# Expert stage of a hybrid mixer and mixture-of-experts layer: matmul order turned, one list for all slots, results added onto x1 in memory

## The reference, cut to what matters

```python
x = x + mod_lat[:, 2] * mix_x                                  # "x1" below
h = modulate(rms_norm(x, norm_ffn_g), mod_lat[:, 3], mod_lat[:, 4])
# router: best group by h @ rg_w + rg_b, then the two best of its four experts by h @ re_w + re_b
for e in range(16):
    y = y + gates[..., e:e + 1] * ((silu(h @ wg[e]) * (h @ wu[e])) @ wd[e])
x = x + mod_lat[:, 5] * y
out = rms_norm(x, final_norm_g)
```

## Time and profile before

| | |
|---|---|
| time, median of 3 runs | 1084.59 us (1083.99 to 1084.71) |
| the profiled execution's own time | 1086.46 us |
| its span, first to last instruction | 1084.7 us |
| mean granted TensorE clock | 0.903 |
| busy: PE, DVE, ACT, POOL | 900.0, 718.8, 415.1, 392.1 us |
| first expert matmul, last `expert_rows` store issued | 536.4, 1028.6 us |

### The profile page before, as it was taken

The page is one execution under the profiler, slowest core; times in us unless marked ns, Lnnn a source line. Parts: engine busy times, 40 slices in busy tenths (PEclk is TensorE's granted clock), DMA queues, the critical chain, the costliest instruction groups (busy, mean ns, idle before and its releaser), DMA issues.

```text
span 1084.7 us, 12383 instructions
## 1 busy us (share of the span) xinstructions
PE 900.0 (83%) x3689; PEld 632.3 (58%) x3690; DVE 718.8 (66%) x794; ACT 415.1 (38%) x520; POOL 392.1 (36%) x181
## 2 busy tenths in 40 slices
PE   6789999949798899992379998999999899988800
PEld 2354444414345478882358886888888677767700
DVE  2234778996883353446885778568646988888648
ACT  1333535325436221113242454435414556556212
POOL 1000735910000000003253647156341777766672
PEclk9989999969899999995589998999999888888955
DMA  8884405015205422316555748476452888887494
GB/s 318 292 330 135 176 20 193 0 39 187 105 0 203 184 78 112 117 78 255 188 190 212 279 168 317 159 271 238 158 223 86 317 317 309 325 311 268 168 358 190
DMA packets 96277, 213.48 MB, mean 197 GB/s; under 512 B 11007, under 2 KB 31613, under 8 KB 96253
## 3 DMA queue, kind: packets, MB, share of 16 engines
q1 hardware_dynamic: 85708, 174.37, 43.9%
q0 software_dynamic: 5904, 21.50, 5.5%
q10 hardware_dynamic: 4640, 17.30, 3.9%
HBM read 180.12 MB, written 33.03 MB: 197 GB/s over the span
## 4 chain that ended last, share of the span: by engine, by line
PE 51%; DVE 28%; issue 8%; DVEq 4%; DMA 3%; ACT 3%; POOL 2%; SPq 0%; ACTq 0%; POOLq 0%
PE bank L701 10%; DVE WP L1524 7%; PE bank L908 3%; PE bank L888 3%; PE bank L887 3%; PE bank L886 3%; PE bank L909 3%; PE bank L910 3%; PE bank L814 3%; PE bank L815 3%; PE bank L816 3%; DVE rkt L1538 2%; PE bank L745 2%; PE bank L683 2%; DVE U L1279 2%
## 5 line engine op out<-in xcount | busy, mean ns | idle before, releaser
L621 POOL TENSOR_TENSOR WP<-raw,WP 128x1024 fp32r<-128x1024 f32 x64 | 186.8, 2947 | 0.7 <-ACT WP L1138 0.5
L701 PE MATMUL bank<-hT,wring 128*128 128x512 f32 x384 | 169.3, 600 | 2.6 <-ACT hT L966 1.9
L1524 DVE TENSOR_TENSOR WP<-raw,WP 128x2048 fp32r<-128x2048 f32 x62 | 156.8, 2568 | 11.7 <-ACT WP L1134 8.3
L1134 ACT ACTIVATE WP<-raw 128x2048 fp32r<-128x2048 f32 x64 | 119.5, 1917 | 90.8 <-issue 84.9
L886 PE MATMUL bank<-WP,xp 128*128 128x512 f32 x368 | 144.1, 391 | 1.5 <-DVE xp L1561 1.5
L888 PE MATMUL bank<-WP,xp 128*128 128x512 f32 x368 | 143.8, 391 | 0.0
L887 PE MATMUL bank<-WP,xp 128*128 128x512 f32 x368 | 143.7, 391 | 0.0
L701 PEld LDWEIGHTS bank<-hT,wring 128*128 128x128 f32 x384 | 73.7, 193 | 93.5 <-issue 90.0
L617 POOL TENSOR_TENSOR held<-held 128x1 f32<-128x1 f32 x24 | 36.2, 1508 | 218.7 <-DVE idg L1553 210.8
L633 POOL TENSOR_TENSOR WP<-raw,WP 128x2048 fp32r<-128x2048 f32 x2 | 9.0, 4532 | 283.6 <-ACT WP L1134 283.6
L908 PE MATMUL bank<-WP,hp 128*128 128x512 f32 x184 | 83.2, 452 | 0.0
(11 more groups left out here) (278 smaller groups left out, 1503.6 us busy)
## 6 DMA issues: line engine op xcount, KB each, us to landing
raw<-in_expert_w_gate SPq DMA_DIRECT2D x64, 512.0 KB, 3.9
raw<-in_expert_w_up SPq DMA_DIRECT2D x64, 512.0 KB, 6.4
raw<-in_expert_w_down SPq DMA_DIRECT2D x64, 512.0 KB, 8.1
mring<-in_mod_w SPq DMA_DIRECT2D x20, 1024.0 KB, 5.3
expert_rows<-ysc ACTq DMA_DIRECT2D x23, 512.0 KB, 7.0
expert_rows<-g SPq DMA_DIRECT2D x16, 512.0 KB, 11.4
wring<-in_w_in SPq DMA_DIRECT2D x12, 512.0 KB, 6.0
mslot<-in_mod_w SPq DMA_DIRECT2D x4, 1024.0 KB, 14.9
```

The source lines that it names most:

```text
L621: pool.tensor_tensor(WP[:, j, 1, 2 * D:], raw[:, j, 2 * D:], WP[:, j, 0, 2 * D:].bitcast(F32), ALU.subtract).then_inc(s_lod[j], 1)
L701: mm = pe.matmul(o_, wring[:, n % 3, k, :], src, start=k == 0, stop=k == KD - 1)
L1134: A_(WP[:, j, 0, 0:2 * D], raw[:, j, 0:2 * D], ACT.Copy).then_inc(s_hgu, 1)
L1524: tt(WP[:, j, 1, 0:2 * D], raw[:, j, 0:2 * D], WP[:, j, 0, 0:2 * D].bitcast(F32), ALU.subtract).then_inc(s_logu[j], 1)
```

## The change

It rewrites the expert stage in five ways.

1. **Lists for all slots at once.** After the ranks are known, DVE computes each pair's slot and place, one one-hot matrix `oh` (128 x 2048 float32) and the values `rv`; 16 float32 matmuls of 70 columns give token numbers and gates of all 35 slots in one PSUM bank. From it come `gid` (rows to gather), `sid` (rows to add to; empty places point to 128 spare rows) and `gl` (gates). `prepare_slots`, `slot_ids`, `slot_gates` and `slot_numbers` are gone from the loop.
2. **PE's order is turned.** `gate_up` of slot q+1 comes before `down` of slot q:

More of the change, by code:

```diff
@@ L528, in _, with next_gate_up, next_down @@
             sp.wait_ge(s_mrow, 8)
+            def next_gate_up(e, at_e):
+                for j in range(KE):
+                    sp.wait_ge(s_logu[j], e)
+                    load_gate_up(at_e, j)
+            def next_down(e, at_e):
+                for j in range(KE):
+                    sp.wait_ge(s_lod[j], e)
+                    load_down(at_e, j)
             for j in range(KE):
@@ L532, in _ @@
                 load_down(0, j)
[L533 to L539, removed]
+            next_gate_up(1, 1)
+            next_down(1, 1)
+            next_gate_up(2, 2)
+            with sp.Fori(2, NE - 1) as e:
+                next_gate_up(e + 1, bass.ds(e + 1, 1))
+                next_down(e, bass.ds(e, 1))
+            next_down(NE - 1, NE - 1)
             for j in range(KE):
@@ L622, in split_down @@
                                    ALU.subtract).then_inc(s_lod[j], 1)
[L624 to L634, removed]
@@ L659, in _ @@
             pool.wait_ge(s_xg, 16 * W + 32)
-            hold(W)
+            scatter(W - 1, 2 * W + 1, xg[:])
+            pool.wait_ge(s_held, 4 * W + 5)
+            pool.tensor_tensor(held[:], held[:], held[:], ALU.mult).then_inc(s_held, 1)
             pool.memset(stat[:, 63:64], 0.0).then_inc(s_end, 1)
[L662 to L667, removed]
@@ L851, in _ @@
                     pe.matmul(bank[4][:, NE * i:NE * (i + 1)], (tri_b if j == i else ones_b)[:],
-                              mb[:, NE * j:NE * (j + 1)], start=j == 0, stop=j == i)
+                              mk[:, NE * j:NE * (j + 1)], start=j == 0, stop=j == i)
             for j in range(NT):
-                mm = pe.matmul(bank[5][:, 0:NE], ones_b[:], mb[:, NE * j:NE * (j + 1)], start=j == 0,
+                mm = pe.matmul(bank[5][:, 0:NE], ones_b[:], mk[:, NE * j:NE * (j + 1)], start=j == 0,
                                stop=j == NT - 1)
             mm.then_inc(s_rk, 1)
[L859 to L868, removed]
+            pe.wait_ge(s_oh, 1)
+            for n in range(2 * NT):
+                mm = pe.matmul(bank[2][:, 0:2 * NS], oh[:, n, :], rv[:, n].rearrange("p f s -> p (f s)"),
+                               start=n == 0, stop=n == 2 * NT - 1)
+            mm.then_inc(s_idx, 1)
             def turn_rows(q, r):
@@ L1143, in hi_rows @@
                    ACT.Copy).then_inc(s_xgh, 1)
-            for n in range(2):
-                act.sem_inc(s_ys[n], 16)
             for j in range(KE):
@@ L1154, in _, with early_hi, late_hi, tanh_and_rows @@
             W = act.value_load(tab[0:1, 3, 0:1], min_val=NE, max_val=MAXT)
+            def early_hi(s, E1):
+                for j in range(KE - 1):
+                    act.wait_ge(s_gud, 4 * s + j + 1)
+                    hi_gate_up(E1, j)
+            def late_hi(s, E1):
+                act.wait_ge(s_gud, 4 * s + 4)
+                hi_gate_up(E1, KE - 1)
+            def tanh_and_rows(s, nxt):
+                act.wait_ge(s_gate, s + 1)
+                A_(sg[:], bank[0][:], ACT.Tanh, scale=0.5).then_inc(s_sg, 1)
+                for r in range(2):
+                    hi_rows(s + 1, nxt, r)
@@ L1572, in _, with hidden @@
-            slot_ids(1)
-            slot_gates(1, 1)
+            def hidden(s):
+                g = gl[:, s:s + 1] if isinstance(s, int) else gl[:, bass.ds(s, 1)]
+                dve.wait_ge(s_sg, s + 1)
+                stt(out=sg[:], in0=sg[:], scalar=1.0, in1=bank[0][:], op0=ALU.add,
+                    op1=ALU.mult).then_inc(s_sil2, 1)
+                dve.wait_ge(s_sil2, s + 1)
+                dve.wait_ge(s_gud, 4 * s + 4)
+                for h in range(2):
+                    hs = slice(h * 2 * P, (h + 1) * 2 * P)
+                    stt(out=sg[:, hs], in0=bank[1][:, hs], scalar=g, in1=sg[:, hs], op0=ALU.mult,
+                        op1=ALU.mult).then_inc(s_hid, 1)
@@ L1584, in _ @@
[L1584 to L1589 removed]
+            for j in range(1, KE):
+                lo_gate_up(0, j)
+            ids1, hole = lst[:, 0], every(1500, NS)
+            link(ts(hole, ids1, 0.0, None, ALU.is_equal))
@@ new lines, in _ @@
+            link(stt(out=hole, in0=hole, scalar=K("dump"), in1=ids1, op0=ALU.mult, op1=ALU.add))
+            ts(sid[:], hole, -1.0, None, ALU.add).then_inc(s_sid, 1)
+            L0 = dve.value_load(tab[0:1, 2, 0:1], min_val=0, max_val=1)
+            E1 = dve.value_load(tab[0:1, 0, 1:2], min_val=0, max_val=NE - 1)
+            W = dve.value_load(tab[0:1, 3, 0:1], min_val=NE, max_val=MAXT)
+            with dve.If(L0 > 0):
+                for j in range(KE - 1):
+                    lo_gate_up(E1, j)
```

422 lines of the change are left out of this document (165 added, 257 removed).

## The result

The changed kernel takes 1097.76 us (median of 4 runs, 1091.22 to 1099.81), the kernel before 1084.65 in the runs beside it: a ratio of 1.011, 95% interval 1.006 to 1.015. It is slower by about 1.1 per cent, where the forecast was 3 per cent faster. The profiled execution took 1097.63.

A forecast was written before the change was run, and what follows sets the result against it. PE was taken to bound the kernel before, POOL the single slots after. Tanh of slot 14 at 796, POOL's last addition done at 1024, plus 27 gave 1051, set as 1050 us; own range 1025 to 1080, whole range 1000 to 1105.

The forecast's parts named there:

- POOL's new chain: Expert loop: POOL waits for each addition to land, so its iteration is a sum, 8 to 26.1 us by slot type.
- the iteration with a new expert after it only: POOL, expert loop: pick and gather 1.6, subtractions 9.5, addition's pick 0.6, addition 8.0, register loads 0.3; 20.0 us.
- PE bounds it: Alternating pairs of slots: 28 to 32 us on POOL against 36 on PE, so PE sets the pace.
- the 238 of the first stretch: Tanh of slot 1 to 14: 13 slots of 18.0 us, 234, plus 4 for the pair 4, 5.
- The single slot: POOL, new expert in both neighbours: 5.5 + 11.7 + 0.6 + 8.0 + 0.3 = 26.1 us, in slots 14 to 21.
- the slow addition: Rival, POOL's wait after 23 additions: landing of 13 us gives 1128, decisive from about 11.3; chance 0.25.
- The start: Before the loop: mask at 503.8, then 23.9 us to the first expert matmul at 527.7, 8.7 earlier than before.
- The tail: From tanh of slot 14 at 796: 19 us, seven iterations of 26.1, one of 20, last addition 6, ending at 1024.
- The end: After POOL's last dummy: the 16 gathers and the additions go, leaving 27 us for 52.5 before.
- A slot that PE bounds: Expert loop: `slot_numbers` goes and DVE's products are covered by `down`; 18.0 us a slot for 18.90.
- The rival with a short chain: Rival, expert loop: POOL's chain is short and PE or the transfers bound all slots; 989 us, chance 0.15.
- DVE bounds the single slots: Rival, single slots: DVE's subtractions and other work take 26 us, or 28 without overlap, giving 1066; chance 0.10.

The follow-up runs named there:

- run 5: Changed kernel, POOL's wait kept, with DVE's gate and up subtractions left out after the first expert: 1025.72 us, ratio 0.945 to the kernel before.
- run 4: Changed kernel with two more idle products of 128 x 560 on POOL after each of 22 additions: 1125.61 us, ratio 1.034 to the kernel before.
- run 8: Changed kernel with POOL waiting for an addition only before the next, and half of the down low parts moved to DVE: 1001.47 us, ratio 0.922.
- run 1: Changed kernel with POOL waiting for an addition only before it issues the next one: 1013.0 us, ratio 0.932 to the kernel before.

## Why the prediction was wrong

The sign was wrong: slower by 1.1 per cent where 3.2 per cent faster was forecast. 1097.76 lies near the upper end of the range from 1000 to 1105, and outside the 1025 to 1080 of the forecast's own case. The mechanism was named: POOL's iteration is a sum, with the landing in it. The step that failed is the sizing of that sum under "POOL's new chain", above all of the iteration with a new expert after it only, 20.0.

**The iteration with a new expert after it only.** It was 1.6 + 9.5 + 0.6 + 8.0 + 0.3 = 20.0, and measured 2.35 + 9.4 + 4.7 + 12.5 = 28.96. I gave the addition's pick 0.6, the uncontended price, and took the landing from the middle of the plain stores. But DVE has its own subtractions of the next expert just then, so both one-element operations wait out one of them (2.30 and 2.13, against 0.18 alone in run 5), and the issue takes 3.52 for 1.62. DVE's three from 579.78 to 587.72 cover all three of these operations (DVE in the changed kernel):

```profile
579.78 7.94 DVE L1523 TENSOR_TENSOR WP<-raw,WP 128x2048 fp32r<-128x2048 f32 x3 [2.97 <-ACT WP L1130]
```

Of the seven iterations before slot 14 that split a new expert's down weights, five take 27.2 to 29.0; the other two, at 655.59 and 795.32, have no subtraction of DVE beside the addition and its pick and take 20.6 and 19.2, as forecast. With the 11.55 of the other iteration (11.1 to 12.1 in four of the five between splits, 17.1 in one, for 8 to 12) a pair takes 40.5 on POOL, not 28 to 32, and that is above PE's 36. So "PE bounds it" failed, and with it the 238 of the first stretch: 261.8 measured, 231.0 where the wait or DVE's subtractions are gone.

**The single slot.** 26.1 was forecast, 28.2 to 30.1 measured in the first five, then 25.7 and 19.4. In the first four the pick is the largest error (2.7 to 4.6 for 0.6), then the addition (9.9 to 11.0 for 8.3); the four subtractions (9.3 to 14.4 for 11.7) are no error in the mean; the first pick and gather took 2.0 to 5.7 for 5.5. The median landing, 8.4, was forecast almost right, and is below the 11.3 from which I had the slow addition decide. That threshold rested on the same sums and fell with them. So the slow-addition rival had the sign, but not by its own mechanism. Its 1128 at a landing of 13 us would have been too low: run 4 reaches 1125.6 with some 2.5 us more per slot on POOL, and 13 is 4.6 above the median, which at the same price is some 50 us more than 1098 (an estimate from run 4).

**The start.** The first expert matmul came at 533.80, not 527.7 (PE and DVE of the changed kernel):

```profile
496.84 3.60 PE L835 MATMUL bank<-rw,h 128*128 128x20 f32 x16 [1.17 <-ACT h L1119]
...
506.37 0.29 DVE L1460 TENSOR_TENSOR mk<-rs 128x128 bf16<-128x128 f32 x1
...
517.47 7.10 PE L861 MATMUL bank<-rv,oh 128*128 128x70 f32 x32 [9.34 <-DVE stat L1501]
...
533.80 0.79 PE L881 MATMUL bank<-WP,xp 128*128 128x512 f32 x1 [1.41 <-DVE xp L1528]
```

The logits came 2.94 later than before. That is scatter: their last group starts between 493.5 and 498.5 in the eleven kernels here, and experiments that change nothing ahead of it lie at both ends. From it to the first expert matmul all changed kernels take 36.8 to 37.1 us, against 42.5 before and 33.8 in the forecast. From the logits on, the mask came after 9.53 us, as forecast (503.8 less 493.9). The matmuls of the lists took 7.10 for my 4.8, near twice the 20-column ones, the upper bound. The tanh of slot 0 came 13.8 after the first matmul, for 11.4. Of the 2.4, about 1.0 is the clock: the first 13 matmuls start some 0.43 us apart, not the first 8 as before. The other 1.4 is ACT: its split of a chunk of the second expert's weights, which had waited 1.72 for its load, ran from 545.78 to 547.70, ahead of the tanh.

**The tail.** From tanh 14 on the forecast was 19 to POOL's iteration 14, seven of 26.1 (183), 20, and 6. Measured from the rows of POOL: 21.5, 190.8, 22.3 and 7.1. The last two have no subtraction of DVE beside them, yet cost more than I gave them. In iteration 21 it is the addition, 10.4 for 8.3. Its low parts of down are made only after an addition has landed, and PE waits 10.2 for them; but DVE had scaled the last y by 1055.33, so the last addition waits for the one before it, not for PE (POOL in the changed kernel).

```profile
1042.96 9.34 POOL L638 TENSOR_TENSOR WP<-raw,WP 128x1024 fp32r<-128x1024 f32 x4 [0.23 <-issue]
...
1052.86 1.63 POOL L632 DMA_INDIRECT mixed_rows<-ysc,idg  x1 [0.16 <-issue]
...
1064.05 1.59 POOL L632 DMA_INDIRECT mixed_rows<-xg,idg  x1 [0.34 <-issue]
1070.34 0.19 POOL L670 TENSOR_TENSOR held<-held 128x1 f32<-128x1 f32 x1 [4.69 <-DMA mixed_rows<-xg,idg]
```

**What held, and the rivals.** The end took 25.5 for 27 (52.5 before). A slot that PE bounds takes 17.3 to 18.2, for 18.0: the turned order hides DVE's products, as the earlier trace rows let expect. The rival with a short chain (989) did not come; run 8, which lacks both the wait and the run of four, reaches 1001. That DVE bounds the single slots at 26 is out: run 1 keeps all of DVE's work and takes 21.0 a slot. By the formula in the Trainium skill ("DMA: Bandwidth & Descriptors", Anatomy of one DMA), an estimate for a transfer of this size from GpSimd is 3.2 us. The trace does not agree for the addition, whose least is 6.1; the plain write's least, 3.4, is near it, but its median is 8.4. The prediction's "never landed under 4.0" holds for the gathers alone: plain stores of that size had landed in 2.6.

## What to carry to other kernels

Where an engine waits for its own transfer, write its iteration as a sum and compare it with the pace of the engine it feeds, at the contention of the place where each term stands: two operations of one element cost 4.4 us here, as they stood beside another engine's long ones. A wait can stay correct one step later, before the next transfer to the same rows, and was worth 85 us here. If an order is turned, turn the loads with it.

## What the runs showed of the hardware

**A run of operations on one engine keeps the other out.** POOL and DVE slow each other, but not evenly. While POOL had four subtractions queued without a wait, one of DVE's stood until all were through (DVE in the changed kernel; POOL's four ran from 883.66 to 893.12):

```profile
880.44 2.29 DVE L1523 TENSOR_TENSOR WP<-raw,WP 128x2048 fp32r<-128x2048 f32 x1 [3.87 <-ACT WP L1130]
883.09 14.39 DVE L1523 TENSOR_TENSOR WP<-raw,WP 128x2048 fp32r<-128x2048 f32 x2 [0.35 <-ACT WP L1130]
```

Two that take 2.28 alone took 14.39; the longest single one 12.19. The Trainium skill ("SBUF — State Buffer", SBUF: two separate sides) has an exclusive lock held for a whole instruction; the rows agree, and show besides that an engine with work queued took it four times running. In the slot before, POOL's four took 13.17 from 852.13 on and DVE's three 10.80 from 858.86 on, so there the two took turns: who gets it differs from slot to slot.

**An addition costs more at the issue too.** The issue for 128 rows of 4 KB took 1.63 us with the addition and 1.01 without, in the median; at most 3.5 and 3.0.
